# First norm summed by rows on ScalarE, key sums behind the scores, a norm factor in bank 4

## The reference

```python
def _rms_norm(x, g):
    xf = x.astype(jnp.float32)
    y = xf * lax.rsqrt(jnp.mean(xf * xf, axis=-1, keepdims=True) + NORM_EPS)
    return (y * g.astype(jnp.float32)).astype(x.dtype)
...
xn = _rms_norm(h, pre_mix_norm[l])
proj = (xn @ w_in[l]).astype(jnp.float32)
...
# in the state-space mixer
scores = jnp.einsum("bclhn,bcshn->bhcls", Ch, Bh)
states = jnp.einsum("bclhn,bhcl,bclhp->bchpn", Bh, decay_states, X)
...
y = y.reshape(b, T, SSD_GROUPS, SSD_D // SSD_GROUPS)
y = y * lax.rsqrt(jnp.mean(y * y, axis=-1, keepdims=True) + NORM_EPS)
...
# in the RWKV mixer
kk = kk / jnp.maximum(jnp.sqrt(jnp.sum(kk * kk, axis=-1, keepdims=True)), 1e-12)
```

## Time and profile before

| | us |
|---|---|
| median of 3 runs | 1830.29 |
| runs, lowest and highest | 1829.9 and 1831.27 |
| profiled execution, its own time | 1828.33 |
| span of that execution, first to last instruction | 1826.5 |
| TensorE busy | 1705.4 |
| VectorE busy | 1208.4 |
| GpSimd busy | 677.0 |
| ScalarE busy | 472.9 |

### The profile page before, as it was taken

The page is one execution under the profiler, slowest core; times in us unless marked ns, Lnnn a source line. Parts: engine busy times, 40 slices in busy tenths (PEclk is TensorE's granted clock), DMA queues, the critical chain, the costliest instruction groups (busy, mean ns, idle before and its releaser), DMA issues.

```text
span 1826.5 us, 29394 instructions
## 1 busy us (share of the span) xinstructions
PE 1705.4 (93%) x12018; PEld 1321.2 (72%) x12018; DVE 1208.4 (66%) x1607; ACT 472.9 (26%) x723; POOL 677.0 (37%) x382
## 2 busy tenths in 40 slices
PE   6999989888979999999879999999999997999998
PEld 4888667776757777777748787778787876666665
DVE  6958686743378888888769148567645525666664
ACT  3111445421021110110141123231231004454452
POOL 2666000001436666666426543426444651000000
PEclk8999899997979999999989999999999999999999
DMA  5223342120242222222212222203221344789884
GB/s 218 93 92 116 113 143 73 49 95 24 70 165 80 92 93 89 92 93 91 92 70 92 93 70 70 70 24 105 98 70 48 109 190 154 306 330 356 322 340 162
DMA packets 34070, 230.54 MB, mean 126 GB/s; under 512 B 4132, under 2 KB 4388, under 8 KB 8232
## 3 DMA queue, kind: packets, MB, share of 16 engines
q1 hardware_dynamic: 30240, 214.48, 32.4%
q10 hardware_dynamic: 2136, 10.24, 1.5%
q0 software_dynamic: 1584, 4.21, 0.7%
HBM read 220.98 MB, written 9.50 MB: 126 GB/s over the span
## 4 chain that ended last, share of the span: by engine, by line
PE 79%; DVE 13%; ACT 3%; DMA 3%; issue 2%; DVEq 0%; SPq 0%; POOL 0%; ACTq 0%; POOLq 0%
PE psum L401 78%; DVE arena L1629 3%; DVE arena L1623 3%; ACT arena L1236 1%; DVE arena L1626 1%; PE psum L405 1%; DMA normed<-units 1%; DMA arena<-units 1%; DVE expert_lo L1623 1%; ACT expert_hi L1236 1%; DVE residual L1623 0%; DVE arena L2241 0%; DMA arena<-x 0%; DVE smalls L2238 0%; DVE tiny L1637 0%
## 5 line engine op out<-in xcount | busy, mean ns | idle before, releaser
L1236 ACT ACTIVATE arena<-psum 128x512 f32<-128x512 f32 (+1 forms) x294 | 148.3, 520 | 829.4 <-PE psum L401 762.4
L401 PE MATMUL psum<-arena 64*64 64x64 f32 (+6 forms) x2820 | 220.6, 265 | 25.8 <-DVE arena L1623 10.8
L401 PEld LDWEIGHTS psum<-arena 64*64 64x64 f32 (+4 forms) x2820 | 149.7, 151 | 81.7 <-issue 49.6
L401 PE MATMUL psum<-normed_hi,w_in_hi 128*128 128x512 f32 x504 | 202.7, 402 | 5.4 <-DVE in_lo L1623 2.8
L401 PE MATMUL psum<-normed_hi,w_in_lo 128*128 128x512 f32 x504 | 200.4, 398 | 0.0
L401 PE MATMUL psum<-in_lo,w_in_hi 128*128 128x512 f32 x504 | 199.0, 395 | 0.0
L1629 DVE SCALAR_TENSOR_TENSOR arena<-arena,fixed_data 128x512 f32<-128x512 f32 x134 | 186.9, 1395 | 13.5 <-DVE arena L1626 0.2
L1623 DVE TENSOR_TENSOR arena<-arena,psum 128x512 f32<-128x512 f32 (+2 forms) x200 | 110.7, 588 | 117.8 <-PE psum L401 72.3
L2488 POOL TENSOR_TENSOR w_ff_lo<-weight_ring,w_ff_hi 128x1024 fp32r<-128x1024 f32 x66 | 167.2, 2533 | 5.5
L2488 POOL TENSOR_TENSOR w_in_lo<-weight_ring,w_in_hi 128x1024 fp32r<-128x1024 f32 x63 | 160.1, 2541 | 5.2
L2486 POOL TENSOR_SCALAR w_in_hi<-weight_ring 128x1024 fp32r<-128x1024 f32 x63 | 72.2, 1146 | 214.2 <-PE psum L401 203.5
(11 more groups left out here) (248 smaller groups left out, 3466.3 us busy)
## 6 DMA issues: line engine op xcount, KB each, us to landing
weight_ring<-units SPq DMA_DIRECT2D x124, 1024.0 KB, 4.8
arena<-units SPq DMA_DIRECT2D x55, 1024.0 KB, 7.7
normed<-units SPq DMA_DIRECT2D x20, 1024.0 KB, 8.4
slots<-arena ACTq DMA_DIRECT2D x7, 516.0 KB, 9.4
arena<-slots SPq DMA_DIRECT2D x7, 516.0 KB, 5.9
fixed_data<-fixed ACTq DMA_DIRECT2D x1, 2944.0 KB, 12.0
arena<-x SPq DMA_DIRECT2D x4, 512.0 KB, 5.8
arena<-bias_rows ACTq DMA_DIRECT2D x2, 896.0 KB, 4.4
```

The lines of the kernel that those rows point to most:

```text
L401: return nc.tensor.matmul(o, l, r, start=start, stop=stop)
L1236: return nc.scalar.activation(o, i, func, **kw)
```

## The change

1. *First norm.* Each piece of x has a semaphore of its own. TensorE transposes piece by piece into all eight banks. ScalarE takes Square of each loaded piece, 128 tokens by 1024 features, with a sum along the row (`accum_out`), so the sum of squares stands in one column per piece, tokens on the partitions. VectorE scales and inverts these 128x4 values, ScalarE takes the root, and TensorE spreads them by products with the identity. The eight squares on VectorE and the column sums on TensorE are gone. ScalarE evacuates tile 4 first (its bank takes the factor), tiles 0 to 2 after the root, and the others between the roundings. The large constants are asked for after tile 2, and the zeroing of the pads stands behind the low parts.
2. *State-space stage.* `prepare(0, 3, 4)` moves behind the score products; the chunk decays move ahead of the state products.
3. *Factor of the first norm group* in bank 4 instead of 5. For pair 0 the transpose of V, which takes bank 4, is issued last, and ScalarE and VectorE follow that order.
4. Two waits of TensorE, for the selector and for the activated c, are dropped.

```diff
+        TM_ORDER = ((t_A, t_BP, t_KP, t_V), (t_A, t_V, t_BP, t_KP))
...
+        X_ORDER = (4, 0, 1, 2, 3, 5, 6, 7)
...
-            pe.wait_ge(sem("x_loaded"), 16 * NT)
-            for k in range(KT):
-                o = open_("x", k, k % 4)
-                for t in range(NT):
-                    last = tr(o[:, t * P:(t + 1) * P], A(XT + t * D + k * P, P))
-                close(last, "x", k)
-            token_sums("sum_pre_mix", [A(SQ + k * T) for k in range(KT)], lambda k: (sem("sq_pre_mix"), k + 1))
-            spread_rs("sum_pre_mix")
+            for k in X_ORDER:
+                open_("x", k, k)
+            for t in range(NT):
+                pe.wait_ge(sem(f"x{t}_loaded"), 16)
+                for k in X_ORDER:
+                    last = tr(PSB[bank_of("x", k)][:, t * P:(t + 1) * P], A(XT + t * D + k * P, P))
+                    if t == NT - 1:
+                        close(last, "x", k)
+            n_rs[0] += 1
+            pe.wait_ge(sem("rstd_ready"), n_rs[0])
+            o = open_(("rs", "sum_pre_mix"), 0, 4)
+            for t in range(NT):
+                last = mm(o[:, t * P:(t + 1) * P], x_rs[:, t:t + 1].to_broadcast([P, P]), C("ident"))
+            close(last, ("rs", "sum_pre_mix"))
...
             prepare(0, 2, 4)
-            prepare(0, 3, 4)
             for g in range(2):
                 o = open_("scores", g, 5 + g)
...
+            prepare(0, 3, 4)
+            o = open_("chunk_decay", 0, 7)
+            for h in range(8):
+                last = mm(o[:, h * NT:(h + 1) * NT], C("sel16", 8, h * P, (h + 1) * P), ym(5, 0, 8)[:, P - 1::P])
+            close(last, "chunk_decay")
...
-            spread_rs("sum_ssd0", 5)
+            spread_rs("sum_ssd0", 4)
...
-            act.wait_ge(sem("x_loaded"), 16 * NT)
+            for t in range(NT):
+                act.wait_ge(sem(f"x{t}_loaded"), 16)
+                f(A(YM + t * D, D), A(XT + t * D, D), ACT.Square, accum_out=x_sums[:, t:t + 1]).then_inc(sem("x_squares"), 1)
+            evac("x", 4, res[:, 4, :])
+            n_rstd[0] += 1
+            act.wait_ge(sem("variance_inverted"), n_rstd[0])
+            f(x_rs, x_rs, ACT.Sqrt).then_inc(sem("rstd_ready"), 1)
+            for k in range(3):
+                evac("x", k, res[:, k, :])
...
-            for k in range(KT):
-                emptied(dve, "x", k)
-                tt(A(SQ + k * T), res[:, k, :], res[:, k, :], ALU.mult).then_inc(sem("sq_pre_mix"), 1)
-
+            dve.wait_ge(sem("x_squares"), NT)
+            link(ts(x_rs, x_sums, 1.0 / D, 1e-6, ALU.mult, ALU.add))
+            n_rstd[0] += 1
+            V.reciprocal(x_rs, x_rs).then_inc(sem("variance_inverted"), 1)
```

More of the change, by code:

```diff
@@ L351, in build @@
         expA = small(1)
+        x_sums, x_rs = dec3[:, 0:NT], dec3[:, NT:2 * NT]
+        X_ORDER = (4, 0, 1, 2, 3, 5, 6, 7)
         one_ka = small(4)
@@ L597, in cs_row @@
                 close(mm(open_("cs_row", h, 5 + h % 2), C("sel16", 8, h * P, (h + 1) * P), ym(5, 0, 8)), "cs_row", h)
-            o = open_("chunk_decay", 0, 7)
-            for h in range(8):
-                last = mm(o[:, h * NT:(h + 1) * NT], C("sel16", 8, h * P, (h + 1) * P), ym(5, 0, 8)[:, P - 1::P])
-            close(last, "chunk_decay")
             cs_row(0)
             cs_row(1)
-            pe.wait_ge(sem("csil_ready"), 1)
             modulation(0)
@@ L663, in _ @@
                 gram("abT", m, (5, 6), ew(e_BH), ew(e_AT))
-                for i, src in ((t_A, ew(e_AT)), (t_V, proj(VV + m)), (t_BP, ew(e_BP)), (t_KP, ew(e_KP))):
+                for i in TM_ORDER[min(m, 1)]:
+                    src = {t_A: ew(e_AT), t_V: proj(VV + m), t_BP: ew(e_BP), t_KP: ew(e_KP)}[i]
                     if i == t_BP:
@@ L1255, in squares_of_x, with round_hi @@
                 n_x[0] += 0 if term else KT
-            def round_hi(tiles, what, shift=None):
+            def round_hi(tiles, what, shift=None, between=None):
                 for k in range(KT):
+                    if between:
+                        between(k)
                     if k < KT - 1:
@@ L1277, in _, with next_x @@
             act.dma_start(fix[:, S0:M0], fixed[:, S0:M0]).then_inc(sem("params_loaded"), 16)
-            act.wait_ge(sem("x_loaded"), 16 * NT)
+            for t in range(NT):
[7 more added lines that the diff above has]
+                evac("x", k, res[:, k, :])
             act.dma_start(fix[:, 2 * P:S0], fixed[:, 2 * P:S0]).then_inc(sem("fixed_loaded"), 16)
             act.dma_start(fix[:, M0:N_FIX], fixed[:, M0:N_FIX]).then_inc(sem("fixed_loaded"), 16)
-            for k in range(KT):
-                evac("x", k, res[:, k, :])
-            rstd()
+            def next_x(k):
+                if k in (0, 1, 2, 3):
+                    m = (3, 5, 6, 7)[k]
+                    evac("x", m, res[:, m, :])
+            round_hi(in1, "sum_pre_mix", None, next_x)
             act.wait_ge(sem("params_loaded"), 16)
-            round_hi(in1, "sum_pre_mix")
-            f(csil[:, :], S("c", 0, KT), ACT.Silu).then_inc(sem("csil_ready"), 1)
+            f(csil[:, :], S("c", 0, KT), ACT.Silu)
             act.wait_ge(sem("pads_zeroed"), 1)
@@ L1365, in _ @@
                 evac("last_decay", m, pls, PSB[bank_of("last_decay", m)][:, 0:8])
-                for t in (t_A, t_V, t_BP, t_KP):
+                for t in TM_ORDER[min(m, 1)]:
                     evac(("tm", m), t, tm(t), four(PSB[bank_of(("tm", m), t)]))
@@ L1645, in _, with scaled_parts @@
             n_hi = [0]
-            def scaled_parts(tiles, what, rs, gain, ready, shift=None):
+            def scaled_parts(tiles, what, rs, gain, ready, shift=None, source=None):
                 for k in range(KT + 2):
                     if k < KT:
+                        if source:
+                            emptied(dve, source, k)
                         stt(tiles.raw(k), res[:, k, :], gain(k), rs, ALU.mult, ALU.mult)\
@@ L1677, in log1p @@
                 link(stt(o, o, 1.0, t1, ALU.add, ALU.mult))
-            for k in range(KT):
-                emptied(dve, "x", k)
-                tt(A(SQ + k * T), res[:, k, :], res[:, k, :], ALU.mult).then_inc(sem("sq_pre_mix"), 1)
+            dve.wait_ge(sem("x_squares"), NT)
+            link(ts(x_rs, x_sums, 1.0 / D, 1e-6, ALU.mult, ALU.add))
+            n_rstd[0] += 1
+            V.reciprocal(x_rs, x_rs).then_inc(sem("variance_inverted"), 1)
+            dve.wait_ge(sem("params_loaded"), 16)
+            filled(dve, ("rs", "sum_pre_mix"))
+            scaled_parts(in1, "sum_pre_mix", PSB[bank_of(("rs", "sum_pre_mix"))], lambda k: S("g_pre_mix", k), "xn_ready",
+                         source="x")
             pv = A(PROJ, N_PROJ * PADW).rearrange("p (t c) -> p t c", c=PADW)
             V.memset(pv[:, :, 0:3], 0.0).then_inc(sem("pads_zeroed"), 1)
-            dve.wait_ge(sem("params_loaded"), 16)
-            rs = rstd("sum_pre_mix", 1.0 / D, 1e-6)
-            scaled_parts(in1, "sum_pre_mix", rs, lambda k: S("g_pre_mix", k), "xn_ready")
             dve.wait_ge(sem("fixed_loaded"), 32)
@@ L1858, in begin_pair @@
                 if m:
-                    filled(dve, ("tm", m - 1), t_KP)
+                    filled(dve, ("tm", m - 1), TM_ORDER[min(m - 1, 1)][3])
                     filled(dve, ("rkT", m - 1), 1)
@@ L2547, in _ @@
             for t in range(NT):
[L2548 removed]
+                sp.dma_start(A(XT + t * D, D), x[t * P:(t + 1) * P, :]).then_inc(sem(f"x{t}_loaded"), 16)
             for u in range(RING):
```

6 lines of the change are left out of this document (1 added, 5 removed).

## The result

The changed kernel took 1810.97 us (median of 4 runs, 1808.56 to 1814.61) beside 1830.10 us of the kernel before in the same comparison (4 runs): a ratio of 0.9897, 95% interval 0.9876 to 0.9917. A later comparison gave 0.9914 (0.9881 to 0.9947). The profiled execution, the fastest of the four, took 1808.56 us (span 1806.8), 19.8 us less than that of before. The forecast was 13.6 us; the sign was right, the size was short by some 6 us, and the median lies 0.03 us outside the low end of the range.

The account below looks back on a forecast made before the run. TensorE, busy in 93% of the span, was taken as the bound, so only its stops pay. Gains of 10.5 + 1.3 + 1.8 = 13.6 us, from a median of 1830.29, gave 1816.7 us, range 1811 to 1821.

Parts of the forecast that it names:

- First norm: Front before the projection: first matmul at 19.7 us instead of 30.2, gaining 10.5 us, bounds 9 and 12.6.
- a sign of being wrong: At the projection's start: a first matmul before 18 or after 21 us would show the forecast wrong.
- Rival (a): First norm: VectorE's first subtraction just precedes GpSimd's last instruction, so no lock wait; gain 15.7 us, time 1814.6, chance 0.17.
- Hidden costs: Constants' transfers leave ScalarE late, masks start up to 3 us late; VectorE's 20.28 us idle in the projection covers it.
- Key sums: State-space stage: scores placed first remove TensorE's 1.36 us stop; gain 1.3 us, bounds 0 and 3.
- Bank 4: Pair 0: gram product no longer waits for the factor's bank; VectorE's idle 1.24 and 0.52 us go, gain 1.8 us.
- Rival (c): State-space clock: staying up gives 1811 us, sinking 8 us more gives 1820.7; chance 0.08 each way.
- (b): First norm: pieces land together, squares pile up, first matmul at 21.4 us; gain 11.9 us, time 1818.4, chance 0.08.
- (d): Projection start: clock stays at 0.50; a loss from 2.4 such tiles on, 1839 us with four; chance 0.02.
- (e): Pair 0: V's late transposes hold the crossed product, leaving 1.2 of 1.8 us; inside the range, no separate chance.

Follow-up runs that it names:

- the changed kernel once more: The changed kernel, unaltered, measured again against the kernel before for the spread of its time: 1809.29 us, ratio 0.9914.
- the bank alone: The kernel before with only the first group's norm factor in bank 4 and V's transpose last for pair 0: 1828.67 us, ratio 0.9998.
- without the bank: The changed kernel with the state-space norm factor back in bank 5, the old transpose order and the two waits restored: 1813.37 us, ratio 0.9916.
- the sums alone: The kernel before with only the key sums moved behind the scores and the chunk decays ahead of the states: 1824.60 us, ratio 0.9977.
- without the norm: The changed kernel with the old first norm (squares on VectorE), the other parts as changed: 1827.24 us, ratio 0.9979 to the kernel before.

## Why the forecast was right, and where it was short

**First norm: forecast 10.5 us, measured 11.5 at P** (11.6 by means: 172.5 over five profiles with this front, 184.0 over four with the old one). The steps stood: squares of 1.06 us and 0.18 for the accumulator (forecast 1.25 together), each over before the next piece lands; root ended at 12.59 (12.65). But the first projection matmul, at 17.15 us, lies before 18, which the prediction itself had named as a sign of being wrong: what stood between root and matmul was mis-sized. The spreading took 1.17 us instead of the 2.09 taken over from the earlier trace rows, since the clock was at 1.00 in it. So the first low part was ready at 15.87 instead of 16.8, and met GpSimd's third instruction, not its fourth. It is the second low part that met the subtraction, and ended at 19.78, where I had the first end at 19.65. The place of the wait was right to 0.15 us, the count of tiles behind it wrong by one, and VectorE's pace of some 1.26 us a tile is the missing 1.0 us. The Trainium skill, SBUF — State Buffer, section "SBUF: two separate sides", says that the pair goes to whoever starts first, for the whole instruction, and counts on VectorE's side operations with two inputs in SBUF. The traces agree on both: 2.20 and 2.19 us with both inputs in SBUF in either form, 0.73 with one in PSUM, and, in quarters, each engine held by the other. Rival (a), that the lock would not bite, is refuted by these rows, though its premise, the spreading at the higher clock, came true.

**Hidden costs: nothing, as forecast.** The larger constants' transfer left at 12.39, together with the root and ahead of the evacuations that stand before it in the stream, not at about 15; it took 9.6 us, not 12, the smaller 13.8. Nor did the two issues hold up ScalarE: the first rounding began at 14.67 instead of 15.8. VectorE waited 0.48 us for them at 26.61, and the cover of the earlier trace rows is still 20.28 us wide (the row at 130.75). No wait of TensorE appeared in the projection after its first tile.

**Key sums: forecast 1.3 us, 0.7 by the fit.** The stop closed as drawn, with 0.21 us left before the scores. The term was mis-sized because I priced the stop and not what follows: TensorE's idle time in the whole stage fell by 1.0 us, not 1.3 (the windows above: 3.4 to 2.4), and of that 0.7 reached the end of the stage.

**Bank 4: forecast 1.8 us, measured 1.5.** The first mask follows the factor's last use without idle time, 1.3 us more shift than at the reciprocal, and the same 1.3 in all ten profiles of kernels with the bank, 0 to 0.25 in the three others; the crossed mask still waits 0.30 us, so 0.2 of its 0.52 went. This second wait depends on the clock during the transposes: it is 1.61 us in the changed kernel once more and in the bank alone, with 6.8 us at 0.50 there, and 1.73 without the bank with as much, and from the reciprocal to this mask 10.38 us with the bank stand against 11.83 without it, so at a like clock the bank is worth 1.45 us. In the comparison of the bank alone this is drowned (0.9998, interval 0.0036 wide).

**The clock: given 0.08, and it decided the size.** Rival (c) priced it at up to 6 us and named 1811, where the median came out. That the median stands at the edge of the range and not clearly below it is luck: two of its four runs lay under 1810, and seven later ones had a median of 1809.29. The step that failed is the weight: the rows of before showed 12 us at 0.50 in this stage and more than one way out of them, and I treated the likeliest time as if the clock were fixed. The fit gives 4.7 us for the stage. Another 1.5 us or so came behind pair 0 (18.3 to 19.8), where the changed kernel's clock was low for some 10 us less up to 450; I did not test that part. The Trainium skill, TensorE: Matmul & The Clock Gate, Part 1, says that matmul activity releases the clock, which pointed to 1811; the four profiles with the stop and nine of the ten without agree in sign, the tenth, the sums alone (20.5 us at 0.50 with the stop closed), shows that the rule does not fix the outcome of one run. The prediction also cites Part 4 for transposes not being counted as such activity. What they did in this stage was not tried, but the start of both kernels speaks against it. In the changed kernel TensorE had done nothing but transposes when the clock record of its trace begins, at 9.36 us, with a rise to 1.00; ahead of that the PEclk of 1.00 in a window has no record behind it. The transposes were 0.21 us apart before and 0.11 behind, as two windows show (4.10 us with 19 of them, 1.50 us with 14):

```profile
5.20:9.30 4.10, 4.10 (x19) 4.10 (x20) 0.00 (x0) 3.21 (x6) 0.00 (x0) 1.00 1.04 421
9.40:10.90 1.50, 1.50 (x14) 1.28 (x12) 0.25 (x2) 1.47 (x3) 0.00 (x0) 1.00 0.99 415
```

In the kernel before the record begins in the same way at 15.33 us, again with nothing but transposes ahead of it.

**Rivals (b), (d) and (e)** did not come: the pieces landed apart (of the 3.0 us of waits, 2.0 stand before the first square and 0.9 between the squares), the projection had 6.8 us at 0.50 at its start and 1.00 from 23 us on (that the clock was up for good from 38.6 us, as the prediction says against (d), holds for the projection alone: the earlier trace rows have 0.50 at 193 and 204 us), and only a part of the 0.6 us of (e) is missing.

## What to carry to other kernels

Before a forecast, add up how long the clock was at its lower level in each stage, and price both ways for it: here 1 us less at 0.50 was worth 0.46 us, and that outweighed two of the three edits. When a serial front is shortened, look what it will newly stand beside, and follow the gain to the end of the stage: of 1.1 us gained at the first matmul by an earlier table, all was still there at the third group and 0.2 at the end of the projection, because TensorE then worked at 0.50 for 3.4 us longer. When a whole run spreads by 10 us, compare landmarks of the trace, and leave parts out rather than adding them up.

## What the runs showed of the hardware

- Within one kernel (without the norm) a run took 1815.36 us at a mean clock of 0.971 and another 1831.41 at 0.961, on one chip; every kernel with six runs or more spread by 8.7 us or more. The clock fell to 0.50 in a stage in which TensorE was 96% busy (61.03 of 63.3 us, sums alone) and with 36 matmuls of a single column (128x1) in it. Transposes alone preceded its first recorded rise in both kernels (9.36 and 15.33 us).
- An instruction of VectorE that reads two tensors from SBUF ended 0.5 to 0.55 us behind the GpSimd instruction that it met, for lengths of 1.04 and 2.68 us; its own plain time was 0.68. With one tensor in PSUM it ran through.
- A root taken first made one table serve squares, copies and the root: two table loads in the first 40 us instead of three (1.28 us each), and the squares kept their 1.06 us.
